# Routing a token layer's experts block by block beside the output projection: router logits taken from the first sublayer's sum

## The chip, the core and the metric

The kernel runs on one core of a Trainium2 chip. The metric is the device time of one execution in microseconds (us). The core has TensorE (PE in the profile; its weight loads are PEld), VectorE (DVE), ScalarE (ACT), GpSimd (POOL) and SyncE (SP), which here only issues transfers. SP and ACT each have a queue of transfers of their own, POOL has one for gathers and scatters.

## The reference, cut to what matters

One layer works on 640 tokens of 1024 numbers: 128 context tokens (modulation vector `c_ctx`) and 512 latent tokens (vector `c`). Sublayer 1 mixes tokens, and sublayer 2 is a mixture of 32 experts of which each token uses two:

```python
sh1, sc1, gt1, sh2, sc2, gt2 = _adaln(c, w_ada[l], b_ada[l])
h = _modulate(xs, g_pre1[l], sh1, sc1)
out, _, _ = _token_mix(h, *mix_w, tabs, cache_ckv[:, l], cache_krope[:, l])
xs = xs + gt1 * _rmsnorm(out, g_post1[l])
h = _modulate(xs, g_pre2[l], sh2, sc2)          # _rmsnorm(x, g) * (1.0 + scale) + shift
xs = xs + gt2 * _rmsnorm(_hier_moe(h, *moe_w), g_post2[l])
...
g_top, g_idx = lax.top_k(g_prob, 1)             # the best of 4 groups
e_top, e_idx = lax.top_k(jax.nn.softmax(e_sel, axis=-1), TOP_K)   # the best 2 of its 8 experts
```

`g_prob` and `e_sel` come from `h @ w_rg + b_rg` and `h @ w_re + b_re`, 4 and 32 columns.

## The kernel before, in words

All arithmetic on TensorE is in 32-bit floats, for which each matmul of the source is two instructions in the profile. The program is one function, `hybrid_layer`, with a block of code for each engine; the engines meet at semaphores. TensorE's work is a list of named groups (`pe_groups`): each takes one of four places of two PSUM banks in turn (n % 4), waits with `begin` until the place's earlier user has been read, and reports with `done`. `landed(eng, name)` waits for a group's end, `free` and `emptied` say and wait that it was read.

The stages: projections, convolution (on DVE) and latent attention up to some 318 us; then, by the list `POST`, the output projection of the five token blocks of 128 (`P0` to `P4`, L1449, 16 matmuls of 512 columns each) with what follows it; then the router's choice; then the experts.

After `P{b}` ACT squares it (L840), DVE scales and adds it to the token rows `x` (L1066, L1068: now x holds the first sublayer's sum), ACT squares that (L849), DVE multiplies by the norm and by `a2`, the scale of sublayer 2 (L1074), and POOL adds the shift `b2` (L568), for the last block DVE (L1079). The result h2 goes to DRAM (L463, L822), from where experts gather it. TensorE transposes it (`ht{b}`, L1270), multiplies by the router's weights (`rt{b}`, L1461) and transposes the logits back (`rl{b}`). These follow the projections by one to three blocks; the last of them come after `P4`. `a2` and `b2` are read from DRAM by SP (L457, L458) once the last attention group `O3` has landed.

When all logits are there DVE picks experts for all five blocks at once in some 45 small steps, each behind a drain (L1104 to L1126), TensorE counts each token's place within its expert (`pos`, L1472), DVE turns the places into one-hot tables (L1145), TensorE makes from them the lists of token numbers (`table0`, L1483), DVE writes them as integers (L1164 to L1169), and POOL gathers the rows of the first pairs of experts (L571). `table1` lists the tokens beyond 64 of an expert.

Experts go in 16 pairs, 64 tokens each: gathered rows are transposed, gate and up matmuls (L1502), silu on ACT, product on DVE, transposes, down matmuls (L1515), copy (L1212), scatter (L576). An expert with more than 64 tokens has extra rounds. A pair's weights (6.3 MB in three pieces) go into one of three slots. SP issues the load of pair p only when pair p - 3 has been used (`w_used`, L1549). Pairs 0 and 1 (without its down piece) are loaded before the projection's end, pair 2 is issued when `P4` has landed, pair 1's down piece when the last h2 is made.

## Time and profile before

| | |
|---|---|
| three runs | 736.33, 736.13, 735.31 us (median 736.13) |
| the profiled execution | 733.19 us, span 731.4 us |
| mean granted TensorE clock | 0.94 |
| PE busy | 592.8 us (81% of the span) |
| DVE, ACT, POOL busy | 267.3, 147.1, 93.8 us |
| chain that ended last | PE 59%, DMA 21%, DVE 7%, issue 5%, ACT 3% |
| moved by DMA | 169.15 MB, mean 231 GB/s |

The span is from the first to the last instruction of the profiled execution. A start time in a row counts from the span's start. A busy share is an average over stages with different limits; what ended the idle time of an engine stands in brackets behind a row of the timeline.

### The profile page before, as it was taken

The numbers are of one execution on the slowest core, as the hardware profiler recorded it, in microseconds if no ns is written. First come the engines' busy times: TensorE is split into PE (matmuls) and PEld (weight loads), VectorE is DVE, ScalarE is ACT, GpSimd is POOL, SyncE is SP. The second block draws the span as 40 slices with busy tenths as digits, with TensorE's granted clock in tenths as the row PEclk, the third lists the DMA queues.
The fourth block names the chain that finished last, engine by engine and source line by source line (L and its number), as shares of the span: only waits on it lengthen the run. The fifth ranks groups of instructions, "written<-read, shape, count | busy, mean of one in ns | idle before, by whom it ended". The sixth has DMA issues, their size and how long they took to land.

```text
span 731.4 us, 8068 instructions
## 1 busy us (share of the span) xinstructions
PE 592.8 (81%) x3086; PEld 304.1 (42%) x3087; DVE 267.3 (37%) x451; ACT 147.1 (20%) x296; POOL 93.8 (13%) x102
## 2 busy tenths in 40 slices
PE   0889899999999999989999267878988777878700
PEld 0656566555555455544455223334333332322200
DVE  2316899998540244402333531101101000100137
ACT  3220000012315444402223102100110000100042
POOL 5000001500000000001110044011111111110015
PEclk9999999999999999999999769989999998999955
DMA  9999935000008510054005720799999999999273
GB/s 334 345 362 369 365 120 198 13 0 1 0 1 353 218 70 1 1 191 181 30 29 228 289 69 30 278 413 405 423 425 424 423 426 427 425 426 407 99 307 144
DMA packets 48548, 169.15 MB, mean 231 GB/s; under 512 B 5642, under 2 KB 14187, under 8 KB 36218
## 3 DMA queue, kind: packets, MB, share of 16 engines
q1 hardware_dynamic: 41216, 156.11, 53.7%
q0 software_dynamic: 6016, 10.96, 4.2%
q10 hardware_dynamic: 1274, 1.52, 0.6%
q8 instruction: 26, 0.43, 0.2%
q14 instruction: 16, 0.13, 0.1%
HBM read 161.48 MB, written 14.44 MB: 241 GB/s over the span
## 4 chain that ended last, share of the span: by engine, by line
PE 59%; DMA 21%; DVE 7%; issue 5%; ACT 3%; PEldq 1%; PEld 1%; DVEq 1%; SPq 1%; ACTq 1%; POOLq 0%
DMA arena<-in_w_up 14%; PE ps L1265 13%; PE ps L1449 9%; PE ps L1502 9%; PE ps L1424 5%; PE ps L1270 4%; PE ps L1515 4%; PE ps L1266 4%; DMA arena<-in_w_ada 3%; PE ps L1433 3%; PE ps L1283 2%; DVE arena L1249 2%; PE ps L1349 2%; DMA x<-in_x_sample 2%; PE ps L1403 1%
## 5 line engine op out<-in xcount | busy, mean ns | idle before, releaser
L1502 PE MATMUL ps<-arena 128*64 128x512 f32 x544 | 129.3, 628 | 22.5 <-DMA arena<-in_w_up 18.0
L1265 PE MATMUL ps<-arena 128*128 128x512 f32 x256 | 131.4, 595 | 1.2 <-issue 1.2
L984 DVE SCALAR_TENSOR_TENSOR arena<-arena 128x655 f32<-128x655 f32 x116 | 95.0, 897 | 0.4 <-issue 0.2
L1502 PEld LDWEIGHTS ps<-arena 128*64 128x64 f32 x544 | 45.5, 145 | 105.1 <-issue 97.2
L1270 PE MATMUL ps<-cst,arena 128*128 128x128 f32 (+2 forms) x349 | 54.7, 300 | 33.0 <-DVE arena L923 17.5
L1515 PE MATMUL ps<-arena 128*64 128x512 f32 x272 | 64.1, 614 | 16.4 <-ACT arena L862 15.8
L1266 PEld LDWEIGHTS ps<-arena 128*128 128x128 f32 x256 | 48.6, 190 | 61.2 <-issue 61.2
L1449 PE MATMUL ps<-arena 128*128 128x512 f32 x160 | 69.2, 593 | 0.9 <-ACT arena L814 0.9
L1270 PEld LDWEIGHTS ps<-cst,arena 128*128 128x128 f32 (+2 forms) x349 | 45.1, 179 | 51.3 <-issue 41.1
L1207 DVE TENSOR_TENSOR arena<-arena,ps 128x256 f32<-128x256 f32 x16 | 6.7, 422 | 132.0 <-ACT arena L867 119.1
L1212 DVE COPY arena<-ps 128x1024 f32<-128x1024 f32 x16 | 19.6, 1225 | 92.6 <-PE ps L1515 92.6
L1266 PE MATMUL ps<-arena 128*128 128x128 f32 (+1 forms) x256 | 50.9, 280 | 0.0
L1449 PEld LDWEIGHTS ps<-arena 128*128 128x128 f32 x160 | 30.2, 190 | 37.9 <-issue 37.9
L867 ACT ACTIVATE arena<-ps 128x256 f32<-128x256 f32 x16 | 6.1, 384 | 191.7 <-PE ps L1502 191.7
L1265 PEld LDWEIGHTS ps<-arena 128*128 128x128 f32 x256 | 39.4, 192 | 2.5 <-issue 2.1
L576 POOL DMA_INDIRECT y_d<-arena,ids x16 | 16.0, 1000 | 187.2 <-DVE arena L1212 186.9
L1424 PE MATMUL ps<-arena 128*128 128x128 f32 (+1 forms) x144 | 39.3, 417 | 0.7 <-ACTq L787 0.7
L568 POOL TENSOR_TENSOR arena<-arena 128x1024 f32<-128x1024 f32 x4 | 9.4, 2342 | 236.4 <-DVE arena L1074 236.4
L1515 PEld LDWEIGHTS ps<-arena 128*64 128x64 f32 x272 | 18.6, 140 | 50.3 <-issue 36.7
L1043 DVE TENSOR_REDUCE amax<-ps 128x1 f32<-128x640 f32 (+1 forms) x20 | 14.3, 717 | 53.9 <-PE ps L1424 53.9
L1424 PEld LDWEIGHTS ps<-arena 128*128 128x128 f32 x144 | 22.5, 191 | 16.8 <-issue 15.3
L862 ACT ACTIVATE arena<-ps 128x1024 f32<-128x1024 f32 (+1 forms) x34 | 22.3, 701 | 33.4 <-PE ps L1270 33.4
(239 smaller groups left out, 523.7 us busy)
## 6 DMA issues: line engine op xcount, KB each, us to landing
arena<-in_w_gate SPq DMA_DIRECT2D x16, 2048.0 KB, 19.8
arena<-in_w_up SPq DMA_DIRECT2D x16, 2048.0 KB, 26.0
arena<-in_w_down SPq DMA_DIRECT2D x16, 2048.0 KB, 30.7
arena<-in_w_ada SPq DMA_DIRECT2D x12, 2048.0 KB, 14.1
arena<-y_d SPq DMA_DIRECT2D x10, 512.0 KB, 7.0
arena<-in_w_in SPq DMA_DIRECT2D x8, 512.0 KB, 13.0
arena<-in_w_out SPq DMA_DIRECT2D x1, 4096.0 KB, 12.9
arena<-ada_d SPq DMA_DIRECT2D x8, 512.0 KB, 10.5
```

The costliest lines, as they stand in the source:

```text
L576: gp.indirect_dma_start(y_d, bass.IndirectOffsetOnAxis(places, 0), src, None, bounds_check=2 * T - 1, oob_is_err=False).then_inc(inc, 16)
L862: return act.activation(dst.rearrange("p k t -> p (k t)"), bank.rearrange("p a b -> p (a b)")[:, 0:count], ACT.Copy)
L984: ins = dve.scalar_tensor_tensor(dst, src, w, dst, ALU.mult, ALU.add)
L1212: dve.tensor_copy(ys[:, s, :], ps[:, 2 + 2 * s:4 + 2 * s, :].rearrange("p a b -> p (a b)")).then_inc(e_ys, 1)
L1265: mm(pp(name)[:, 0:TS], lhs(k), rhs_s(k), start=k == 0, stop=k == steps - 1)
L1266: last = mm(pp(name)[:, 512:512 + width], lhs(k), rhs_p(k), start=k == 0, stop=k == steps - 1)
L1270: return nc.tensor.transpose(out, in_, ident[0:n, 0:n])
L1424: last = mm(g[:, lo:hi], a[:, h, cols], keys, start=m == 0, stop=m == 1)
L1433: mm(g[:, 0:TS], vv[:, 1 + t, n * DV:(n + 1) * DV], pT[:, t, :], start=t == 0, stop=t == 4)
L1449: last = mm(pp(name)[:, half * 512:(half + 1) * 512], mixT[:, k, b * P:(b + 1) * P], wo[:, k, half * 512:(half + 1) * 512], start=k == CM, ...
L1502: last = mm(ps[a:a + ROWS, s, :], src[:, k, a:a + ROWS], slots[w][:, j, 0:2, k * FE:(k + 1) * FE], start=k == 0, stop=k == KD - 1)
L1515: last = mm(ps[a:a + ROWS, 2 + 2 * s + half, :], src[:, k, a:a + ROWS], slots[w][:, j, 2, k * D + half * 512:k * D + (half + 1) * 512], st ...
```

## The change

It computes the router's logits from x, the sum of the first sublayer, instead of from h2. Since h2 = x * r * a2 + b2, with r the row's norm factor, the logits are r * (x @ (a2 * w)) + (b2 @ w + bias). POOL multiplies the router's weights by a2 beforehand, once per modulation vector (`wr0` for block 0, `wr` for the others); TensorE turns a2 and b2 into columns (group `turn34`, after `q1`), multiplies b2 by the weights (`rb`), and spreads the result over 128 partitions (`small`, ahead of `P0`), from where DVE copies it (`biasrow`). So that rows match, the router's weights are read as (k p) instead of (p k).

`P0` to `P4` alternate between places 0 and 1, `ht` keeps place 3, and place 2 holds logits, places, counts and tables. Transposes of x, logits, the choice of experts, the places and the tables now go one block at a time, put between the matmuls of the next projection; the last projection is done column half by column half. The token numbers are built in PSUM with 4096 as a start value, so that DVE's conversion is two operations. ACT makes the numbers. POOL adds b2 for all five blocks; ACT issues the last store. Pair 1's and pair 2's down pieces are loaded after the second gather has landed; the gather of pair 3 is issued in pair 0 instead of pair 1. The wait for `cnt_ready` moves from ahead of pair 0 to behind its down matmuls.

The diff, cut to its core:

```diff
-POST = ["P0", "P1", "P2", "ht0", "P3", "rt0", "ht1", "P4", "rl0", "rt1", "ht2", "ht3", "rl1", "rt2", "rl2", "rt3",
-        "rl3", "ht4", "rt4", "rl4"]
-
-BETWEEN = (("rl0", "rt1", "ht2"), ("ht3", "rl1", "rt2", "rl2", "rt3", "rl3"))
+POST = ["small", "P0", "P1", "ht0", "P2", "ht1", "P3", "ht2", "P4", "ht3", "ht4"]
+HOME = {"small": 2, **{f"P{b}": b % 2 for b in range(NT)}, **{f"ht{b}": 3 for b in range(NT)}}
...
-            load_pair(2, 2)
-            sp.wait_ge(h2_last, 1)
+            load_pair(2, 2, pieces=range(2))
+            sp.wait_ge(h2_ready, NT)
+            sp.wait_ge(xg_in[1], 16)
             load_pair(1, 1, pieces=range(2, 3))
-
+            load_pair(2, 2, pieces=range(2, 3))
...
+            emptied(gp, "rb")
+            gp.wait_ge(proj_dve, 1)
+            gp.tensor_tensor(wr0, wr[:], a2T[:, :, 0:1].broadcast_to([P, KD, G + E]), ALU.mult)
+            gp.tensor_tensor(wr[:], wr[:], a2T[:, :, 1:2].broadcast_to([P, KD, G + E]), ALU.mult)
+            for v in range(2):
+                last = gp.tensor_scalar(diag[:, v, :], ident[0:G + E, 0:G + E], lgb[:, v:v + 1], None, ALU.mult)
+            last.then_inc(wr2_ready, 1)
...
-                if 0 < pair < PAIRS - 2:
+                if pair == 0:
+                    gp.wait_ge(e_tr, 2)
+                    gather(xg[:, 1, :], idg[:, 0, 3:4], xg_in[1])
...
-            act.dma_start(x_rg, i["w_rg"][0].rearrange("(p k) e -> p k e", k=KD)).then_inc(wr_in, 16)
-            act.dma_start(x_re, i["w_re"][0].rearrange("(p k) e -> p k e", k=KD)).then_inc(wr_in, 16)
+            act.dma_start(x_rg, i["w_rg"][0].rearrange("(k p) e -> p k e", p=P)).then_inc(wr_in, 16)
+            act.dma_start(x_re, i["w_re"][0].rearrange("(k p) e -> p k e", p=P)).then_inc(wr_in, 16)
...
+            dve.wait_ge(bias_in, 1)
+            dve.tensor_copy(biasrow, bias_ps).then_inc(bias_ready, 1)
...
+                if n == 1:
+                    begin(pe, "turn34")
+                    pe.wait_ge(rows_ready, 5)
+                    for a in range(4):
+                        last = turn(pp("turn34")[:, a * P:(a + 1) * P], rows[:, 6 + a, :])
+                    done(last, "turn34")
...
+            pe.wait_ge(wr_ready, 1)
+            begin(pe, "rb")
+            for k in range(KD):
+                last = mm(pp("rb")[0:G + E, 0:2], wr[:, k, :], b2T[:, k, :], start=k == 0, stop=k == KD - 1)
+            done(last, "rb")
```

The new code of DVE between the projections (`step` is a drain; the last block, done in halves, is left out):

```python
            def route(b):
                v = min(b, 1)
                Lg, Le = L[:, 0:G], L[:, G:]
                best0, best1, best2 = (m[:, b:b + 1] for m in (m0, m1, m2))
                dve.wait_ge(lg_done, b + 1)
                step(dve.scalar_tensor_tensor(L, lg_ps[:, b, :], stat[:, 7, b:b + 1], biasrow[:, v, :], ALU.mult, ALU.add))
                first_best(pen, Lg, hitg, best0, rankg, 1e30)
                step(dve.scalar_tensor_tensor(em.rearrange("p (g e) -> p g e", g=G), pen.unsqueeze(2).broadcast_to([P, G, EG]), -1e30,
                                              Le.rearrange("p (g e) -> p g e", g=G), ALU.add, ALU.add))
                first_best(oh[:, 0, b, :], em, hit, best1, ranke)
                step(dve.scalar_tensor_tensor(em, oh[:, 0, b, :], -2e30, em, ALU.mult, ALU.add))
                first_best(oh[:, 1, b, :], em, hit, best2, ranke)
                dve.tensor_scalar(rt_e[:, b, 0:G], Lg, best0, None, ALU.subtract).then_inc(mask_ready, 1)
                dve.tensor_tensor(rt_e[:, b, G:], best2, best1, ALU.subtract)
            def find(b):
                dve.wait_ge(pos_done, b + 1)
                for c in range(2):
                    dve.scalar_tensor_tensor(junk[:, c, :], pos_ps[:, b, :], 1.0, oh[:, c, b, :], ALU.mult, ALU.mult, accum_out=at[:, c, b:b + 1])
                dve.drain()
                for c in range(2):
                    last = dve.tensor_scalar(place1[:, c, b, :], iota, at[:, c, b:b + 1], None, ALU.is_equal)
                last.then_inc(place_ready, 1)
            for b in range(NT - 1):
                v = min(b, 1)
                name = f"P{b}"
                dve.wait_ge(pss, b + 1)
                dve.tensor_tensor(po[:], pp(name), gg1[:, v, :], ALU.mult)
                dve.wait_ge(psd, b + 1)
                step(dve.reciprocal(stat[:, 5, b:b + 1], stat[:, 5, b:b + 1]))
                free(dve.scalar_tensor_tensor(x[:, b, :], po[:], stat[:, 5, b:b + 1], x[:, b, :], ALU.mult, ALU.add), name)
                dve.drain().then_inc(x1_ready, 1)
                if b:
                    find(b - 1)
                dve.wait_ge(xsd, b + 1)
                step(dve.reciprocal(stat[:, 7, b:b + 1], stat[:, 7, b:b + 1]))
                if b >= 2:
                    dve.wait_ge(h2_st[b % 2], 16 * (b // 2))
                dve.scalar_tensor_tensor(h2[:, b % 2, :], x[:, b, :], stat[:, 7, b:b + 1], a2[:, v, :], ALU.mult, ALU.mult).then_inc(h2m_ready, 1)
                if b == NT - 2:
                    dve.wait_ge(pss, NT)
                    dve.tensor_tensor(po[:, 0:512], pp(f"P{b + 1}")[:, 0:512], gg1[:, 1, 0:512], ALU.mult)
                    dve.tensor_scalar(stat[:, 1, b + 1:b + 2], stat[:, 0, b + 1:b + 2], 1.0 / D, EPS, ALU.mult, ALU.add).then_inc(rest_ready, 1)
                route(b)
            find(NT - 2)
...
```

The new code of TensorE (turn_rows is 8 transposes of x, logits 8 matmuls of 36 columns, places 2(b+1) and table 8 small ones in bf16; each waits for what its name needs, table(n, b) for number_ready):

```python
            begin(pe, "small")
            pe.wait_ge(wr2_ready, 1)
            for v in range(2):
                last = mm(bias_ps[:, v, :], ones[0:G + E, :], diag[:, v, :], start=True, stop=True)
            last.then_inc(bias_in, 1)
            pe.wait_ge(wo_in, 16)
            pe.wait_ge(bias_ready, 1)
...
            for b in range(NT):
                name = f"P{b}"
                begin(pe, name)
                if b == 0:
                    for h in range(H):
                        emptied(pe, f"O{h}")
                tiles = (*range(CM, KD), *range(CM))
                if b < NT - 1:
                    steps = [(k, half) for k in tiles for half in range(2)]
                else:
                    steps = [(k, half) for half in range(2) for k in tiles]
                for n, (k, half) in enumerate(steps):
                    if b == 0 and k == 0:
                        pe.wait_ge(mixc_ready, CM)
                    if b >= 2 and n == 2:
                        pe.wait_ge(place_ready, b - 1)
                        table(0, b - 2)
                    if b and n == 6:
                        turn_rows(b - 1)
                    if b and n == 9:
                        logits(b - 1)
                    if b and n == 15:
                        places(b - 1)
                    last = mm(pp(name)[:, half * 512:(half + 1) * 512], mixT[:, k, b * P:(b + 1) * P],
                              wo[:, k, half * 512:(half + 1) * 512], start=k == CM, stop=k == CM - 1)
                    if b == NT - 1 and n == 7:
                        last.then_inc(p_half, 1)
                done(last, name)
            turn_rows(NT - 1)
            pe.wait_ge(place_ready, NT - 1)
            table(0, NT - 2)
            logits(NT - 1)
            places(NT - 1)
            pe.wait_ge(place_ready, NT)
            table(0, NT - 1)
            for a in range(NT):
                for c in range(2):
                    last = mm(cnt_ps, onesb[:], oh[:, c, a, :], start=a == c == 0, stop=a == NT - 1 and c == 1)
            last.then_inc(cnt_done, 1)
            pe.wait_ge(place_ready, NT + 1)
            for b in range(NT):
                table(1, b)
```

How TensorE's order changes at the start of the projection. Before, from the last matmul of `O3` (L1434) on into `P0`, `P1` and `P2` (L1449):

```order
L1434 MATMUL ps<-arena 128x128
L1449 MATMUL ps<-arena 128x512 [waits drained1,drained2,drained0,wr_ready,wo_in]
L1449 MATMUL ps<-arena 128x512 x7
L1449 MATMUL ps<-arena 128x512 [waits mixc_ready]
L1449 MATMUL ps<-arena 128x512 x7
```

The same place in the change (L1505 is the end of `O3`, L1583 is `P0`):

```order
L1505 MATMUL ps<-arena 128x128
L1510 MATMUL ps<-cst,ones 128x36 [waits wr2_ready,drained2]
L1510 MATMUL ps<-cst,ones 128x36
L1583 MATMUL ps<-arena 128x512 [waits drained3,drained0,drained2,bias_ready,wo_in]
L1583 MATMUL ps<-arena 128x512 x7
L1583 MATMUL ps<-arena 128x512 [waits mixc_ready] x2
```

And DVE's side of it in the change, between the last attention step (L1110) and the first block's scaling (L1163):

```order
L1110 TENSOR_SCALAR arena<-arena,asum 128x128
L1116 COPY cst<-ps 128x72 [waits b2_in,bias_in,a2_in,gg1_in]
L1163 TENSOR_TENSOR arena<-ps,arena 128x1024 [waits pss]
L1165 RECIPROCAL stat<-stat 128x1 [waits psd]
L1166 SCALAR_TENSOR_TENSOR x<-arena,stat,x 128x1024
```

`P0` now waits for `bias_ready`, which that copy gives, and the copy waits for the loads of a2 and b2.

TensorE in the change from the end of `P1` (L1583) to the logits of block 1; before, sixteen rows of L1449 stood here with nothing between them:

```order
L1543 MATMUL ps<-arena,trib 128x32 [waits mask_ready]
L1543 MATMUL ps<-arena,trib 128x32
L1583 MATMUL ps<-arena 128x512
L1583 MATMUL ps<-arena 128x512 [waits drained0]
L1583 MATMUL ps<-arena 128x512
L1552 MATMUL ps<-padb,onesb 64x16 [waits number_ready,place_ready]
L1555 MATMUL ps<-number,place 64x16 x4
L1552 MATMUL ps<-padb,onesb 64x16
L1555 MATMUL ps<-number,place 64x16 x4
L1583 MATMUL ps<-arena 128x512 x4
L1329 MATMUL ps<-cst,x 128x128 [waits x1_ready,drained3]
```

And DVE in the change after `P1` has landed, up to where it gives `place_ready` for block 0 (second instruction of L1156):

```order
L1163 TENSOR_TENSOR arena<-ps,arena 128x1024 [waits pss]
L1165 RECIPROCAL stat<-stat 128x1 [waits psd]
L1166 SCALAR_TENSOR_TENSOR x<-arena,stat,x 128x1024
L1153 SCALAR_TENSOR_TENSOR arena<-ps,arena 128x32 [waits pos_done]
L1153 SCALAR_TENSOR_TENSOR arena<-ps,arena 128x32
L1156 TENSOR_SCALAR place<-cst,arena 128x64 x2
```

The table of block b - 2 stands behind two matmuls of `P{b}`, and on DVE the place of that block stands behind the scaling of `P{b-1}`.

## Rows read from the trace of the kernel before

**Rows 1.** The page: PE's busy tenths in 40 slices of the span.
```profile
PE   0889899999999999989999267878988777878700
```
**Rows 2.** Timeline of PE at the projections: start, length, engine, line, count, [idle before].
```profile
319.13 31.14 PE L1449 MATMUL ps<-arena 128*128 128x512 f32 x72 [0.95 <-ACT arena L814]
...
375.11 1.94 PE L1461 MATMUL ps<-arena,wr 128*36 128x128 f32 x16
376.98 1.16 PE L1270 MATMUL ps<-cst,arena 128*128 128x128 f32 x8
377.98 13.90 PE L1449 MATMUL ps<-arena 128*128 128x512 f32 x32
```
**Rows 3.** Timeline of SP at attention's end; then L458's issues, us to landing.
```profile
318.21 0.32 SPq L457 DMA_DIRECT2D arena<-ada_d  x1
...
319.52 0.43 SPq L458 DMA_DIRECT2D arena<-ada_d  x1
...
DMA to landing us min/median/max: 5.1/6.2/7.3
```
**Rows 4.** Timeline of DVE and POOL after P3's end at 375.11.
```profile
376.36 0.15 DVE L1062 TENSOR_SCALAR stat<-stat 128x1 f32<-128x1 f32 x1 [8.19 <-ACT arena L840]
...
377.02 1.28 DVE L1066 SCALAR_TENSOR_TENSOR arena<-ps,stat,arena 128x1024 f32<-128x1024 f32 x1
...
382.87 2.35 POOL L568 TENSOR_TENSOR arena<-arena 128x1024 f32<-128x1024 f32 x1 [12.27 <-DVE arena L1074]
```
**Rows 5.** Timeline from the choice of experts to the first expert matmuls.
```profile
407.78 0.17 DVE L1104 TENSOR_REDUCE arena<-cst 128x5 f32<-128x20 f32 x1 [7.00 <-ACT cst L831]
408.03 0.18 DVE L1105 TENSOR_TENSOR arena<-cst,arena 128x20 f32<-128x20 f32 x1
...
418.91 0.72 PE L1483 MATMUL ps<-number,place 128*64 128x32 bf16 x20 [3.12 <-DVE place L1145]
...
421.44 0.18 DVE L1169 TENSOR_TENSOR idg<-arena 128x16 int32<-128x16 f32 x1
...
422.49 1.10 POOL L571 DMA_INDIRECT arena<-h_d,idg  x1 [37.28 <-DVE idg L1169]
...
423.33 0.17 DVE L1181 TENSOR_REDUCE arena<-arena 1x16 f32<-1x32 f32 x1
...
425.98 0.17 DVE L1164 COPY arena<-ps 128x32 f32<-128x32 f32 x1
...
427.00 1.94 PE L1270 MATMUL ps<-cst,arena 128*128 128x128 f32 x8 [2.71 <-DMA arena<-h_d,idg]
...
430.14 9.35 PE L1502 MATMUL ps<-arena 128*64 128x512 f32 x32 [1.20 <-ACT arena L862]
```
**Rows 6.** The page's DMA issues of h2 (count, KB, us to landing), and ACT's queue (packets, MB, share).
```profile
h_d<-arena SPq DMA_DIRECT2D x4, 512.0 KB, 2.6
...
h_d<-arena ACTq DMA_DIRECT2D x1, 512.0 KB, 8.4
...
q10 hardware_dynamic: 1274, 1.52, 0.6%
```
**Rows 7.** Stretches: length, busy PE, PEld, DVE, ACT, POOL, clock, DMA share, GB/s.
```profile
25.00:30.00 5.00, 3.55 (x108) 3.00 (x99) 1.32 (x4) 0.59 (x2) 0.00 (x0) 1.00 0.78 255
...
525.00:550.00 25.00, 22.28 (x108) 8.52 (x106) 2.84 (x4) 3.36 (x6) 3.23 (x4) 1.00 1.01 424
```
**Rows 8.** Timeline of SP and PE among the experts: pair 3's load, and a late gather.
```profile
461.67 0.39 SPq L429 DMA_DIRECT2D arena<-in_w_gate  x1
...
485.62 2.22 PE L1270 MATMUL ps<-cst,arena 128*128 128x128 f32 x10 [3.31 <-DMA arena<-h_d,idg]
```
**Rows 9.** Timeline of PE: gate and up matmuls of a pair after stops of three lengths.
```profile
580.05 7.34 PE L1502 MATMUL ps<-arena 128*64 128x512 f32 x32 [2.90 <-DMA arena<-in_w_up]
...
613.30 9.94 PE L1502 MATMUL ps<-arena 128*64 128x512 f32 x32 [3.44 <-DMA arena<-in_w_up]
...
646.46 8.72 PE L1502 MATMUL ps<-arena 128*64 128x512 f32 x32 [3.29 <-DMA arena<-in_w_up]
```

More of the change, by code:

```diff
@@ L503, in _ @@
             gp.memset(ids[:], PAD)
+            gp.memset(padb[:], float(PAD // P))
             gp.memset(rows, 0.0)
@@ new lines, in _ @@
+            find(NT - 2)
+            b = NT - 1
+            name = f"P{b}"
+            dve.wait_ge(pss, NT + 1)
+            dve.tensor_tensor(po[:, 512:], pp(name)[:, 512:], gg1[:, 1, 512:], ALU.mult)
+            dve.wait_ge(psd, NT)
+            step(dve.reciprocal(stat[:, 5, b:b + 1], stat[:, 5, b:b + 1]))
+            for half in range(2):
+                part_ = slice(512 * half, 512 * (half + 1))
+                ins = dve.scalar_tensor_tensor(x[:, b, part_], po[:, part_], stat[:, 5, b:b + 1], x[:, b, part_], ALU.mult, ALU.add)
+                if half:
+                    free(ins, name)
+                    dve.drain().then_inc(x1_ready, 1)
+                else:
+                    ins.then_inc(x1_ready, 1)
@@ L1184, in _ @@
             step(dve.tensor_scalar(extra[:, 0:PAIRS], extra[:, 0:PAIRS], ROWS.bit_length() - 1, None, ALU.arith_shift_right))
-            runs = [rt[0:1, 8, 2 * n * PAIRS:2 * (n + 1) * PAIRS] for n in range(2)]
-            dve.memset(rt[0:1, 8, 0:4 * PAIRS], 0.0)
-            step(None)
+            for run in runs:
+                last = dve.memset(run, 0.0)
+            step(last)
             step(dve.tensor_copy(runs[0][:, PAIRS:], extra[:, 0:PAIRS]))
@@ new lines, in logits, with places @@
+            def logits(b):
+                if b == NT - 1:
+                    pe.wait_ge(xT_half, 1)
+                else:
+                    emptied(pe, f"ht{b}")
+                for k in range(KD):
+                    if b == NT - 1 and k == KD // 2:
+                        emptied(pe, f"ht{b}")
+                    last = mm(lg_ps[:, b, :], x1T[:, k, :], (wr if b else wr0)[:, k, :], start=k == 0, stop=k == KD - 1)
+                last.then_inc(lg_done, 1)
+            def places(b):
+                pe.wait_ge(mask_ready, b + 1)
+                steps = [(trib if a == b else onesb, c, a) for a in range(b + 1) for c in range(2)]
+                for n, (w, c, a) in enumerate(steps):
+                    last = mm(pos_ps[:, b, :], w[:], oh[:, c, a, :], start=n == 0, stop=n == len(steps) - 1)
+                last.then_inc(pos_done, 1)
@@ new lines, in table @@
+            def table(n, b):
+                pe.wait_ge(number_ready, b + 1)
+                for j in range(2):
+                    at_rows = slice(j * ROWS, (j + 1) * ROWS)
+                    if b == 0:
+                        mm(tables[n][at_rows], onesb[:, 0:ROWS], padb[:], start=True, stop=False)
+                    for c in range(2):
+                        for kind in range(2):
+                            last = mm(tables[n][at_rows], place1[:, c, b, :], number[:, c, b, kind, j::2],
+                                      start=False, stop=c == kind == 1 and b == NT - 1)
+                if b == NT - 1:
+                    last.then_inc(tab_done, 1)
@@ L1488, in _ @@
+            for b in range(NT):
+                table(1, b)
             for s in range(4):
-                n = sum(1 for name in order if place[name][0] == s)
+                n = homes.count(s) - (s == HOME["small"])
                 pe.wait_ge(drained[s], n)
```

397 lines of the change are left out of this document (186 added, 211 removed).

## The prediction

> **What bounds the kernel now.** I read the page first, then the chain of waits, then the timeline of each engine from the end of attention to the first expert, and last the expert stage by stretches. The page's PE row shows TensorE full from the fifth slice to the twentieth and at the ninth tenth again in slices 16 to 21, with one hole, the slice with a 2 [rows 1]. That hole is the router's choice. In it the chain leaves TensorE and runs over DVE, TensorE, DVE, POOL's gather and back. Ahead of it TensorE streams the five output projections almost without a stop: 0.4325 us for each of 160 instructions (31.14 / 72), 13.84 us a block [rows 2]. So whatever is put between them on TensorE is paid in full.
>
> Behind the hole the experts' weights decide. SP issues pair 3's load at 461.67, when pair 0 is used up [rows 8], and from about there DMA is full at 424 GB/s [rows 7]. Thirteen pairs of 6.3 MB have to pass after that moment, so the end of the kernel moves with the start of pair 0, one to one. That start is 430.14 now, 38.3 us after `P4`'s end at 391.88 [rows 2, 5]. All I have to find is when pair 0 starts.
>
> **The change, part by part.** *Ahead of the projections.* `turn34` adds four transposes, at 1.16 / 8 = 0.145 us each 0.6 us [rows 2]. `rb` adds 16 instructions with 2 moving columns. The nearest row takes 1.94 / 16 = 0.12 us with 128 columns; I take half of it, 0.9 us, with nothing and 1.9 as bounds. Both stand in the full stretch [rows 1]: **+1.5**. The copies on ACT and the three small POOL jobs (two products of 288 columns, the diagonals) run under attention, where POOL stands idle; without that cover they would cost about 2 us.
>
> The router's weights now arrive in runs of 16 and 128 bytes, 2048 of them for 256 before. ACT's queue had 1274 packets in 0.6% of 16 engines' span, 55 ns each, so 1792 more cost at most 6 us of DMA [rows 6]. DMA has room just after, a share of 0.78 from 25 to 30 us [rows 7]. I take 0 and keep +4 for the range. The Trainium skill (DMA: Bandwidth & Descriptors, section Why small descriptors are slow) speaks against such runs; by it this load alone would be slower, which no row here shows.
>
> *The wait ahead of P0.* `P0` starts at 319.13 now, once ACT has read `O3` [rows 2]. In the change TensorE first waits for `bias_ready`, DVE's copy, and that copy stands behind DVE's waits for a2 and b2. SP issues these loads at 318.21 to 319.52 and can't sooner, since it waits for `O3` as well; the last of b2 lands up to 7.3 us after issue, at 326.8 [rows 3]. Before, nobody needed them until the first block was squared 14 us later. With 0.3 us for the copy `P0` starts 8.0 us late: **+8.0**. With the shortest landing, 5.1, it would be 5.8. Queued behind this wait is all of TensorE's projection, and all engines wait for that.
>
> TensorE then comes out of 9 us without work. The first expert matmuls, which start after such a hole, took 9.35 us [rows 5], against 7.34 after a short stop [rows 9]. **+2.0** (1.4 to 2.6, rows 9's other two).
>
> *Work put into the projections.* Before, 72.75 us from `P0`'s start to `P4`'s end less 5 x 13.84 leave 3.55 for transposes and logits [rows 2]. Now four blocks have 1.16 for transposes and 1.94 for logits (16 instructions as before, with 128 weight columns and 36 moving instead of the reverse; between 1.0 and 2.2 by the transposes' row), 12.4 us. 20 small matmuls for places and 26 for tables at 0.72 / 20 = 0.036 us [rows 5] add 1.7. Net **+10.5** (7 to 12).
>
> *The wait for a place in the table.* `table(0, b-2)` stands behind the second matmul of `P{b}`, 4 x 0.4325 = 1.73 us after `P{b-1}` has ended. It waits for `place_ready` of block b - 2, which DVE gives only behind the scaling of block b - 1. By rows 4 DVE starts 1.25 us after a projection ends; a product of 1.28, reciprocal and drain 0.25, a second product of 1.28, a drain of 0.15, and four small operations of the place, 0.7, give 4.9 [rows 4]. TensorE stands for 3.15 us in each of `P2`, `P3` and `P4`: **+9.5** (8.4 to 10.5). After it nothing else is late: transposes, ACT's copy, logits and choice each are ready 1 us or more ahead of their turn.
>
> Does a stop of 3.15 us cost the clock? In rows 9 a stop of 2.90 us is followed by 7.34 us, one of 3.29 by 8.72, one of 3.44 by 9.94. Mine lies between the first two, nearer to the one that loses 1.4. I take 0.7 each: **+2.1**, with 0 and 3 x 2.6 = 7.8 as bounds. The Trainium skill (TensorE: Matmul & The Clock Gate, Part 1: The HAM clock gate) says that an idle TensorE falls to half its clock, and that the moment at which it changes varies from run to run. By that each stop could lose 2.6 and the sum below would be 5.7 higher.
>
> *The tail.* With T the end of `P4`: half a row squared, 0.75; scaled and added, 2.35 and 3.0 for the two halves (each 0.65, half of 1.28); squares' sum 4.0; ACT's root behind its two copies 4.65; h2 without shift 6.25 [rows 4]. The choice is 15 drained steps of 0.25 us [rows 5], to 10.3. Places 0.5, DVE's table 0.7, eight matmuls and latency 0.5, the integers 0.45: 12.45, and POOL issues the gather 0.85 later as from 421.62 to 422.49 [rows 5], at 13.3. The store of h2 has to be there too: POOL's add takes 2.35 [rows 4], so it is issued at 9.1 and lands 2.6 to 8.4 later [rows 6]. Pair 2's first 4.2 MB, issued at T, take 10 us at 424 GB/s, so I expect it at 13.3 as well. The gather lands at 17.8 (422.49 to 427.00). TensorE is not ready then: `table1` now stands ahead of the transposes, behind DVE's counting (2.65 us from 423.33 to 425.98, plus 0.45 for a copy and a memset), two big comparisons 1.15, and 42 small matmuls 1.5 [rows 5], to 18.5. Add 3.14 (427.00 to 430.14) and pair 0 starts at T + 21.7, not T + 38.3: **-16.6** (-19 to -13).
>
> *Among the experts.* The moved gather of pair 3 removes a stop of 3.3 us at 485.62 [rows 8]. DMA was full through it, so the loads gain nothing: 0. The down pieces moved behind the second gather (4.2 MB, 10 us) are done 20 us before pair 0 is used up: 0. If they were late, pair 1 would wait.
>
> **The sum.** 1.5 + 8.0 + 2.0 + 10.5 + 9.5 + 2.1 - 16.6 = +17.0 us. The profiled execution had 733.19, so 750.2; the median of the runs shown is 2.94 above it, so I forecast **753.1 us**, own range 747 to 759.
>
> **The rivals.** A: each stop of `P2` to `P4` falls fully to the half clock. For it: rows 9. Against it: my stop is the shortest but one. +22.7, 758.8 us.
>
> B: the expert stage is bound by TensorE early on, not by DMA, and the earlier gather gives back 3.3 us and about 2.5 of slow clock behind it. Against: the DMA share of 1.01. +11.2, 747.3 us.
>
> C, the other side: neither wait shows. `P0` isn't held because b2 is there before `O3` has been read, and the place of a block is ready within 1.73 us of the next landing. Then only work and tail count: 1.5 + 10.5 - 16.6 = -4.6, 731.5 us. For it: the shorter tail is real. Against: SP's issue and DVE's order, both fixed in the program. It decides where `bias_ready` comes before 319.4 and `place_ready` before T' + 1.7.
>
> D: the small runs of the router's weights delay the first chunks: +4 more, 757 us.
>
> **How the numbers follow.** Forecast 0.56, A 0.15, B 0.12, C 0.06, D 0.06, others 0.05. The range 742 to 764 leaves out C and the far ends. About 0.2% (1.5 us) is what a measurement tells from no change. Faster 0.07 (C and a little), same 0.02, slower 0.91.
>
> **What would show it.** In the changed profile `P0` (L1583) starts near 328.6 with an idle of some 9 us ended by DVE's copy L1116; three stops of about 3 us ahead of L1552 or L1555, ended by DVE L1156; `P4` ends near 425.5; the gather (L611) is issued 13 us later; pair 0 starts 22 us after `P4`'s end, and from it on the stage takes as long as before. I am wrong if `P0` starts before 322, if those stops are under 1 us, or if the span from pair 0's start to the end changes by over 3 us.

## The result, and the profile after

The changed kernel takes 756.71 us (median of 4 runs, 755.28 to 760.35), the kernel before 735.72 beside it: ratio 1.030, interval 1.027 to 1.032. The forecast was 753.1 with a range of 742 to 764. The profiled execution took 757.97 with a span of 756.2, so 24.8 more than the profiled one of before, where the sum had +17.0. Between the medians the change costs 21.0: the profiled execution of before lay 2.5 under the median of its four, the profiled one of the change 1.3 above. The table below splits up the 24.8 of the two profiles.

First the page. The columns are 40 slices of the span, as in [rows 1]: busy tenths of PE, then the granted clock in tenths.

```profile
PE   0889899999999999859888848888987787787700
...
PEclk9999999999999999979989957999998999898955
```

The hole of [rows 1], the 2 and the 6, has become one slice with a 4, the 24th. It is shorter, as meant. In its place the stretch ahead of it, from the 18th slice on, has a 5 and eights where nines stood. These are the new waits. The timeline of PE names them (start, length, engine, line, operation, count, idle before it and what ended that):

```profile
322.13 0.63 PE L1510 MATMUL ps<-cst,ones 36*128 36x36 f32 x4 [0.85 <-ACT arena L862]
330.43 21.46 PE L1583 MATMUL ps<-arena 128*128 128x512 f32 x44 [7.67 <-issue]
...
368.12 0.20 PE L1552 MATMUL ps<-padb,onesb 128*64 128x16 bf16 x1 [3.13 <-DVE place L1156]
...
368.43 5.40 PE L1583 MATMUL ps<-arena 128*128 128x512 f32 x8
...
390.45 0.40 PE L1555 MATMUL ps<-number,place 128*64 128x16 bf16 x8 [3.48 <-DVE place L1156]
390.78 6.57 PE L1583 MATMUL ps<-arena 128*128 128x512 f32 x8
...
413.68 0.39 PE L1555 MATMUL ps<-number,place 128*64 128x16 bf16 x8 [3.12 <-DVE place L1156]
414.00 5.21 PE L1583 MATMUL ps<-arena 128*128 128x512 f32 x8
...
429.64 1.10 PE L1583 MATMUL ps<-arena 128*128 128x512 f32 x2
433.24 1.51 PE L1329 MATMUL ps<-cst,x 128*128 128x128 f32 x8 [2.50 <-DVE x L1191]
...
435.01 3.63 PE L1535 MATMUL ps<-wr,arena 128*128 128x36 f32 x16
443.58 0.40 PE L1543 MATMUL ps<-arena,onesb 128*128 128x32 bf16 x8 [4.94 <-DVE arena L1146]
...
452.37 1.94 PE L1329 MATMUL ps<-cst,arena 128*128 128x128 f32 x8 [1.05 <-DMA arena<-h_d,idg]
455.51 5.39 PE L1617 MATMUL ps<-arena 128*64 128x512 f32 x12 [1.20 <-ACT arena L918]
```

`P0` (L1583) starts 7.67 us after the bias matmuls. "Issue" stands there because DVE's copy is so short. DVE's own timeline has it, behind a wait for the load of a2 and b2:

```profile
330.10 0.23 DVE L1116 COPY cst<-ps 128x72 f32<-128x72 f32 x1 [16.44 <-DMA arena<-ada_d]
```

Then come three stops of 3.1 to 3.5 us ahead of the tables, and behind each, eight instructions of projection in 5.2 to 6.6 us instead of 8 x 0.4325 = 3.5 [rows 2]. The stretches (columns as in [rows 7]) tell why they are slow:

```profile
331.00:335.00 4.00, 4.00 (x6) 1.52 (x5) 0.00 (x0) 0.00 (x0) 0.00 (x0) 0.50 1.01 426
...
368.00:374.00 6.00, 5.88 (x22) 2.79 (x23) 1.51 (x3) 0.64 (x3) 2.34 (x1) 0.72 0.08 33
390.00:397.00 7.00, 6.54 (x16) 2.97 (x17) 1.85 (x4) 0.98 (x3) 2.34 (x1) 0.53 0.19 74
413.00:420.00 7.00, 6.32 (x25) 3.48 (x26) 2.00 (x8) 1.20 (x3) 2.34 (x1) 0.76 0.14 57
434.00:452.00 18.00, 7.23 (x98) 6.41 (x97) 11.55 (x69) 3.81 (x9) 4.63 (x3) 0.50 0.70 264
```

The third number from the end is the granted clock: 1.00 is 2.4 GHz and 0.50 is 1.2 GHz; a value between them is the mean of a stretch that holds both. It is 0.53 to 0.76 behind the three stops, and 0.50 in the tail from 434 us on. What holds the place back is DVE's order around the first stop, as the prediction had it: block 1's product and scaling stand ahead of the place of block 0, whose last comparison (L1156) releases TensorE.

```profile
364.46 1.23 DVE L1163 TENSOR_TENSOR arena<-ps,arena 128x1024 f32<-128x1024 f32 x1 [2.81 <-ACT arena L874]
...
365.83 1.28 DVE L1166 SCALAR_TENSOR_TENSOR x<-arena,stat,x 128x1024 f32<-128x1024 f32 x1
...
367.65 0.42 DVE L1156 TENSOR_SCALAR place<-cst,arena 128x64 bf16<-128x64 f32 x2
```

Against [rows 5], pair 0 now starts 24.8 us after `P4`'s end at 430.74, not 38.3. It starts at 455.51 instead of 430.14, and from there to the end of the span it is 300.7 us against 301.3. SP issues pair 3's load 31.8 us after pair 0's start, 31.5 before [rows 5, 8].

The 24.8 us by the prediction's terms, each from these rows or from an experiment below:

| term | forecast | measured |
|---|---|---|
| ahead of attention's end | +1.5 | +3.1 (321.31 against 318.21), mostly scatter |
| wait ahead of P0 | +8.0 | +8.2 (9.12 from SP's issue of a2 to P0, against 0.92) |
| clock behind it | +2.0 | +2.3 |
| work among the projections | +10.5 | +9.0 |
| three stops | +9.5 | +9.7 |
| clock behind them | +2.1 | +6.1 |
| tail | -16.6 | -13.5 |
| experts | 0 | -0.6 |

They add to 24.3; 0.5 lies in the gaps between the groups.

### The profile page after: what moved, and what is told of

It reads as the page before. It is cut to its first block and busy times, and to the rows that moved or that the text cites. A ratio compares the mean times of both kernels' runs of the same rounds, so it can differ in the third digit from the quotient of the medians.

```text
span 756.2 us, 8386 instructions
## 1 busy us (share of the span) xinstructions
PE 609.3 (81%) x3169; PEld 309.4 (41%) x3170; DVE 277.0 (37%) x538; ACT 151.0 (20%) x311; POOL 97.8 (13%) x108
## 3 DMA queue, kind: packets, MB, share of 16 engines
q10 hardware_dynamic: 3066, 1.52, 0.7%
## 5 line engine op out<-in xcount | busy, mean ns | idle before, releaser
L1617 PE MATMUL ps<-arena 128*64 128x512 f32 x544 | 133.6, 648 | 24.4 <-DMA arena<-in_w_up 19.5
L1324 PE MATMUL ps<-arena 128*128 128x512 f32 x256 | 132.1, 598 | 1.1 <-issue 1.1
L1617 PEld LDWEIGHTS ps<-arena 128*64 128x64 f32 x544 | 43.0, 148 | 113.8 <-issue 110.6
L1583 PE MATMUL ps<-arena 128*128 128x512 f32 x160 | 80.6, 656 | 7.7 <-issue 7.7
L1630 PE MATMUL ps<-arena 128*64 128x512 f32 x272 | 62.1, 598 | 16.9 <-ACT arena L918 15.9
L1325 PEld LDWEIGHTS ps<-arena 128*128 128x128 f32 x256 | 48.8, 191 | 61.5 <-issue 61.5
L1329 PE MATMUL ps<-cst,arena 128*128 128x128 f32 (+1 forms) x313 | 48.5, 297 | 26.7 <-DVE arena L981 17.5
L1329 PEld LDWEIGHTS ps<-cst,arena 128*128 128x128 f32 (+1 forms) x313 | 40.0, 176 | 43.7 <-issue 39.4
L1583 PEld LDWEIGHTS ps<-arena 128*128 128x128 f32 x160 | 32.4, 211 | 43.5 <-issue 43.4
L616 POOL DMA_INDIRECT y_d<-arena,ids x16 | 15.8, 989 | 195.1 <-DVE arena L1271 185.7
L1324 PEld LDWEIGHTS ps<-arena 128*128 128x128 f32 x256 | 39.6, 193 | 2.7 <-issue 2.3
L1630 PEld LDWEIGHTS ps<-arena 128*64 128x64 f32 x272 | 18.1, 136 | 49.2 <-issue 35.6
L607 POOL TENSOR_TENSOR arena<-arena 128x1024 f32<-128x1024 f32 x5 | 11.7, 2342 | 198.1 <-DVE arena L1174 179.1
L1495 PEld LDWEIGHTS ps<-arena 128*128 128x128 f32 x144 | 22.5, 191 | 16.8 <-issue 15.3
## 6 DMA issues: line engine op xcount, KB each, us to landing
arena<-in_w_in SPq DMA_DIRECT2D x8, 512.0 KB, 12.8
arena<-in_w_out SPq DMA_DIRECT2D x1, 4096.0 KB, 12.6
arena<-ada_d SPq DMA_DIRECT2D x8, 512.0 KB, 10.3
```

Of the source, the lines that this page charges most:

```text
L616: gp.indirect_dma_start(y_d, bass.IndirectOffsetOnAxis(places, 0), src, None, bounds_check=2 * T - 1, oob_is_err=False).then_inc(inc, 16)
L1324: mm(pp(name)[:, 0:TS], lhs(k), rhs_s(k), start=k == 0, stop=k == steps - 1)
L1325: last = mm(pp(name)[:, 512:512 + width], lhs(k), rhs_p(k), start=k == 0, stop=k == steps - 1)
L1329: return nc.tensor.transpose(out, in_, ident[0:n, 0:n])
L1495: last = mm(g[:, lo:hi], a[:, h, cols], keys, start=m == 0, stop=m == 1)
L1583: last = mm(pp(name)[:, half * 512:(half + 1) * 512], mixT[:, k, b * P:(b + 1) * P], wo[:, k, half * 512:(half + 1) * 512], start=k == CM, ...
```

## The experiments

**One wait alone.** DVE copies the bias row first.

```diff
-            dve.wait_ge(gg1_in, 32)
-            dve.wait_ge(a2_in, 32)
-            dve.wait_ge(b2_in, 32)
             dve.wait_ge(bias_in, 1)
             dve.tensor_copy(biasrow, bias_ps).then_inc(bias_ready, 1)
+            dve.wait_ge(gg1_in, 32)
+            dve.wait_ge(a2_in, 32)
+            dve.wait_ge(b2_in, 32)
```

> The changed kernel with one edit: DVE copies the bias row ahead of its waits for gg1, a2 and b2, so TensorE's bias_ready no longer hangs on those loads. Theory (the wait ahead of P0 and the slow clock behind it are both its doing): P0's first matmul starts near 322.5 instead of 330.43 and P0 takes 13.9 us instead of 16.3, so the time falls by 8 + 2.5 = 10.5 us, to about 746 us. Rival (P0 is slow because of the two small matmuls and the single-precision work before it, not the idle): P0 still takes 16 us, the time falls by 8 us only, to about 749. Second rival (the b2 load is waited for elsewhere, by DVE's scaling of block 0): under 4 us fall. The three stops for place_ready stay at 3.1 to 3.5 us in all of these.

743.36 us, ratio 1.0116 (1.0088 to 1.0144): 13.4 us below the changed kernel. PE's timeline:

```profile
322.72 0.63 PE L1510 MATMUL ps<-cst,ones 36*128 36x36 f32 x4 [0.85 <-ACT arena L862]
323.72 19.12 PE L1583 MATMUL ps<-arena 128*128 128x512 f32 x44 [0.37 <-issue]
...
359.07 0.20 PE L1552 MATMUL ps<-padb,onesb 128*64 128x16 bf16 x1 [3.13 <-DVE place L1156]
```

The wait is gone and the 44 instructions take 19.12 instead of 21.46, so the slow clock was the wait's doing: 2.3 us. `P0` starts 1.8 us after SP's issue of a2, 0.9 more than before the change: that much of the 8.2 are the two bias matmuls. The stops stand as they were, at 3.13, 3.48 and 3.12 us, and the groups behind them take 5.40, 6.25 and 5.05 us. The wait and its clock explain 9.6 us. The two profiled executions are 12.7 apart, and 3.0 of that lie behind pair 0's start (297.7 us to the end), in a stage that this edit does not touch and that varies by as much from run to run (below).

**The stops alone.** DVE makes the place ahead of the square's wait.

```diff
                 name = f"P{b}"
+                if b:
+                    find(b - 1)
                 dve.wait_ge(pss, b + 1)
...
                 dve.drain().then_inc(x1_ready, 1)
-                if b:
-                    find(b - 1)
```

> The changed kernel with one edit: in the block loop DVE makes the place of block b-1 before it waits for the square of projection b, not after block b is scaled. Theory (stops and the slow clock behind them belong together, rival A of the prediction): the three stops of 3.13, 3.48 and 3.12 us go, and the eight instructions behind them take 3.5 us instead of 5.4, 6.6 and 5.2, together 9.7 + 6.8 = 16.5 us less, about 740 us. Rival (the slow clock comes from the many small matmuls of tables and places between the projections): 9.7 us less, about 747. Second rival (the place is then late for another reason, since places(b-1) ends only 0.4 us before the projection): DVE's scaling starts later, under 8 us less.

738.95 us, ratio 1.0065 (1.0042 to 1.0089): 17.8 below the changed kernel. All three stops are gone, and behind each table there is now

```profile
361.86 3.70 PE L1583 MATMUL ps<-arena 128*128 128x512 f32 x8
...
378.87 3.70 PE L1583 MATMUL ps<-arena 128*128 128x512 f32 x8
```

at a granted clock of 1.00. Against 3.70, the groups of the changed kernel lost 1.7, 2.9 and 1.5 us. The small matmuls of places and tables are still there, so they don't lower the clock; the stops do. Rival A's mechanism was right, and most of its size: 6.1 of the 7.8 us that it took for three stops.

**Both edits together**, measured twice.

> Both edits together. Theory (the two waits and their clock are the whole loss): 10.5 + 16.5 = 27 us less than the changed kernel, about 730 us, so 6 us (0.8%) faster than the kernel before. Rival (with the waits gone another wait takes their place, DVE or ACT as the bound of the block loop): over 734. From pair 0's start to the end 300 to 302 us either way.

730.22 us, ratio 0.9939 (0.9919 to 0.9960). The second time:

> e3_both_early once more, in more rounds, beside the other three: 0.994 of the kernel before. If it is within 0.2% of it, the first result was scatter of the part ahead of the projections, which came out at 318 or at 321 us in kernels whose code is the same up to there.

729.79 us, ratio 0.9927 (0.9898 to 0.9956). So 27 us of loss were two orders of DVE's instructions, and without them the change is 0.6 to 0.7% faster than the kernel before: small, but both intervals end below 1. This kernel also gives the price of the work alone: from `P0`'s start at 319.30 to `P4`'s end at 401.07 it is 81.77 us, against 72.75 [rows 2], so 9.0.

**The wait alone in the kernel before.**

```diff
                             emptied(pe, f"O{h}")
+                        pe.wait_ge(b2_in, 32)
```

> The kernel before with one wait added and nothing else: TensorE waits for the b2 load ahead of P0. Theory: P0 starts 7.5 us late (by the landing at 326.8 instead of 319.13) and runs its first instructions at the lower clock, 2.5 us more: +10, about 746 us. Rival (no clock is lost behind such a hole): +7.5, about 743. Second rival (the expert stage gives it back, since its end is set by the weight loads and not by pair 0's start): under +4.

743.45 us, ratio 1.0106 (1.0071 to 1.0141), 8.9 more than before. Its row:

```profile
328.87 44.09 PE L1450 MATMUL ps<-arena 128*128 128x512 f32 x96 [8.21 <-DMA arena<-ada_d]
```

The idle of 8.21 was 0.95 before [rows 2], and 96 instructions at 0.4325 take 41.5: 7.3 + 2.6 = 9.9, and the interval is 5 to 10 us. Nothing downstream gives the wait back: from pair 0's start to the end it is 301.2 us, 301.3 without the added wait.

**The tail: traffic.** Here and below the edits stand on the kernel with both early edits. Pair 2's loads wait for the last h2 store:

```diff
             landed(sp, f"P{NT - 1}")
+            sp.wait_ge(h2_st[0], 16 * 3)
             load_pair(2, 2, pieces=range(2))
-            sp.wait_ge(h2_ready, NT)
```

> The kernel with both early edits (e3_both_early), and pair 2's gate and up loads issued only when the last h2 store has landed. There the gather was issued at 417.88, 1.3 us after its indices; ready indices alone gave 0.87 in the kernel before. Theory (the store, slowed by these 4.2 MB, ended last): the store lands in about 3 us instead of 6.6, the gather is issued 0.45 us earlier, pair 0 starts 0.45 us earlier, the time falls by 0.5 us, under what can be measured. Rival (the loads come too late for pair 2): pair 2's gate and up waits, over 1 us slower.

734.05 us, ratio 0.9999 (0.9973 to 1.0025): 4 us slower than both edits alone. Neither theory had the reason, which the timelines of SP, POOL and PE show:

```profile
413.34 0.38 SPq L457 DMA_DIRECT2D arena<-in_w_gate  x1
...
417.57 1.14 POOL L611 DMA_INDIRECT arena<-h_d,idg  x1 [7.13 <-DVE idg L1213]
...
426.57 1.94 PE L1329 MATMUL ps<-cst,arena 128*128 128x128 f32 x8 [4.15 <-DMA arena<-h_d,idg]
```

The store landed 2.8 us after its issue at 410.47 and the gather was issued 0.4 us earlier after `P4`'s end, as the theory had it, but now 4.2 MB lay in front of it. From the gather's issue to TensorE's start it took 9.0 us, against 4.5 in [rows 5] and in the kernel with both edits. Pair 0 started 28.5 us after `P4`'s end instead of 24.5. The loads don't hold up the gather when they are issued at `P4`'s end, some 16 us ahead of it: with both edits alone the last of them lands at 415.88, and the gather is issued at 417.88.

With the loads behind both gathers instead, and pair 1's down pieces first:

```diff
             landed(sp, f"P{NT - 1}")
-            load_pair(2, 2, pieces=range(2))
             sp.wait_ge(h2_ready, NT)
             sp.wait_ge(xg_in[1], 16)
             load_pair(1, 1, pieces=range(2, 3))
-            load_pair(2, 2, pieces=range(2, 3))
+            load_pair(2, 2)
```

> The kernel with both early edits (e3_both_early), and pair 2's gate and up loads issued behind both first gathers, after pair 1's down pieces, so that neither the last h2 store nor the gather has other traffic beside it. 8.4 MB at 424 GB/s need 20 us, to 445, and pair 2 reads them at 456, so they should not be missed. Theory (in e6_store_first the loads collided with the gather, which landed 4.2 us later): the gather lands as in e3_both_early or 0.5 us earlier, the time is within 1 us of it, about 730. Rival (e6_store_first was slow because pair 2's loads came late): again 4 us slower.

729.28 us, ratio 0.9926 (0.9901 to 0.9950), as both edits alone. The gather was issued 16.4 us after `P4`'s end instead of 16.8 and was no longer waited for, since `table1`, which stands ahead of the transposes, ended as late. So the store that lands last in the tail costs under half a microsecond.

**The tail: clock.** Extra matmuls into a free bank fill TensorE's waits.

```diff
+            def keep_busy(count):
+                for _ in range(count):
+                    mm(ps[:, 2, :], ident, x[:, 0, 0:512], start=True, stop=True)
+            emptied(pe, f"P{NT - 2}")
+            keep_busy(5)
             turn_rows(NT - 1)
...
             logits(NT - 1)
+            keep_busy(9)
             places(NT - 1)
...
             last.then_inc(cnt_done, 1)
+            keep_busy(7)
             pe.wait_ge(place_ready, NT + 1)
```

> The kernel with both early edits, and 21 extra matmuls of 128x512 in a free bank in the tail: 5 ahead of the last block's transposes, 9 behind its logits, 7 behind the counts, each group meant to end before the wait that follows it. Theory (idle stops of 2.5 to 5 us put TensorE at half its clock): logits of block 4 take 1.9 us instead of 3.63, the transposes of pair 0 1.04 instead of 1.94, its gate and up 7.1 instead of 9.48. The gather gains nothing from the logits, since the h2 store ends last: 0.9 + 2.4 = 3.3 us less, about 727. Rival (half clock comes from the kind of work, or the extra matmuls themselves run at half clock and hold up the places): no fall, up to 3 us more. Second rival (the expert stage is bound by the weight loads whose first issue depends on pair 0's end): the whole 3.3 us arrives, for that is what the theory says; if it were bound by loads alone from pair 0 on, 0.

727.94 us, ratio 0.9922 (0.9896 to 0.9947). The experiment was sized badly: each call is two instructions, so the first group ran 4.3 us in a wait of 2.5, and pair 0 started 26.3 us after `P4`'s end, later and not earlier. The time came out as forecast (727), but not by way of the tail. Why it is no longer than with both edits alone stays unexplained: 298.5 us from pair 0 on is among the shorter ones. The same groups with the store first:

> Both of the last two edits. Theory: now the shorter logits count too, since the gather no longer waits for the store: 1.7 + 0.9 + 2.4 + 0.45 = 5.4 us less than e3_both_early, about 725. Rival (store not what holds the gather): as e7_warm.

734.97 us, ratio 1.0012 (0.9989 to 1.0035): the gather collides with pair 2's loads again. With the loads late and groups of 3, 5 and 4:

> As e10_loads_late, with extra matmuls in the tail again, now 3, 5 and 4: in e7_warm each turned out to be two instructions of 0.43 us, so its groups of 5, 9 and 7 ran 1.5 to 3 us over the waits they were to fill. Theory (each idle stop costs clock behind it, and the groups now fit): pair 0 starts 21.5 us after P4's end instead of 24.5 (1.7 from the logits, 0.9 from the transposes, 0.5 from the store), and its gate and up take 7.1 us: 5.5 us less than e3_both_early, about 725. Rival (the extra matmuls still delay what follows): as e7_warm, 728 or more.

727.77 us, ratio 0.991 (0.9889 to 0.9931), the best here, though its interval overlaps that of both edits alone, so a gain of the clock is not shown by the time. The tail's clock, first with both edits alone, where `P4` ended at 401.07:

```profile
404.00:414.00 10.00, 5.40 (x32) 4.90 (x30) 5.63 (x21) 1.56 (x5) 2.34 (x1) 0.50 1.00 413
414.00:424.00 10.00, 4.21 (x78) 3.83 (x78) 7.06 (x56) 2.46 (x6) 2.16 (x2) 0.50 0.34 100
```

then here, where it ended at 403.53, and two rows of PE:

```profile
404.00:414.00 10.00, 9.82 (x47) 5.23 (x45) 7.95 (x18) 2.65 (x8) 2.34 (x1) 1.00 0.11 46
414.00:424.00 10.00, 5.83 (x81) 3.38 (x82) 7.15 (x50) 2.46 (x6) 2.16 (x2) 1.00 0.27 83
```

```profile
407.47 1.97 PE L1534 MATMUL ps<-wr,arena 128*128 128x36 f32 x16
...
426.00 8.72 PE L1624 MATMUL ps<-arena 128*64 128x512 f32 x32 [1.21 <-ACT arena L917]
```

The clock is whole from `P4`'s end to 424 us, the logits take 1.97 instead of 3.63, and pair 0 starts 22.5 us after `P4`'s end. The theory's 21.5 was too good, and gate and up took 8.72 instead of 9.5, not 7.1: they start behind pair 0's transposes and a wait of 1.21 us that no group fills, and there the granted clock is 0.50 again (426 to 428 us).

**The last block's halves.** The last projection writes both halves in turn again, its first product stands behind block 3's place, and the numbers of block 3 ahead of the first square.

```diff
-                if b < NT - 1:
-                    steps = [(k, half) for k in tiles for half in range(2)]
-                else:
-                    steps = [(k, half) for half in range(2) for k in tiles]
+                steps = [(k, half) for k in tiles for half in range(2)]
...
-                    if b == NT - 1 and n == 7:
+                    if b == NT - 1 and n == 14:
```

> The kernel with both early edits, without one part of the change: the last projection again writes both halves in turn, so ACT squares and DVE scales its first half after P4's end and not beside it. Theory: one half square (0.75 us) and one half product (0.65 us) come back on the path in part, pair 0 starts 25.2 to 26 us after P4's end instead of 24.5, about +1 us. Rival (the halves are hidden by the wait for the h2 store): 0.

729.07 us, ratio 0.9913 (0.9883 to 0.9944). Pair 0 starts 24.65 us after `P4`'s end; in the two profiles of both edits it was 24.46 and 24.73. Computing the last projection half by half gives nothing that shows. The halves behind it, of x and its transposes, are still there in this run and were not tried.

**Pair 3's gather** back behind pair 0's scatter:

```diff
-                if pair == 0:
-                    gp.wait_ge(e_tr, 2)
-                    gather(xg[:, 1, :], idg[:, 0, 3:4], xg_in[1])
-                elif 1 < pair < PAIRS - 2:
+                if 0 < pair < PAIRS - 2:
```

> The kernel with both early edits, pair 3's gather back behind pair 0's scatter as in the kernel before. Theory (the stage is bound by its weight loads, so the moved gather gives nothing): the stop of 3.3 us in front of pair 3's transposes comes back, the time stays within 1 us. Rival B of the prediction (bound by TensorE there): 3 to 6 us slower.

733.31 us, ratio 0.9981 (0.9958 to 1.0005): 3 us slower than both edits alone, with intervals that barely touch. The theory, which allowed 1 us, missed. PE and SP:

```profile
483.93 2.20 PE L1326 MATMUL ps<-cst,arena 128*128 128x128 f32 x10 [4.43 <-DMA arena<-h_d,idg]
487.08 5.63 PE L1627 MATMUL ps<-arena 128*64 128x512 f32 x16 [0.96 <-ACT arena L915]
```

```profile
492.98 0.37 SPq L457 DMA_DIRECT2D arena<-in_w_gate  x1
```

A stop of 4.43 us, then a down that takes 5.63 instead of 3.65, and SP issues pair 5's load 64.8 us after pair 0's start. With both edits alone that issue is at 483.24, 57.7 us after it. Pairs 3 and 4 are 12.6 MB, 29.7 us at 424 GB/s, from the issue of pair 3's load at 458.93 to some 489, so DMA runs short before the next load comes. The stretches show it, here and then with both edits alone, as far from pair 0's start:

```profile
490.19:494.19 4.00, 3.53 (x16) 0.96 (x14) 1.23 (x1) 0.00 (x0) 0.00 (x0) 0.88 0.93 365
494.19:500.19 6.00, 6.00 (x30) 1.84 (x26) 0.00 (x0) 0.00 (x0) 2.02 (x2) 1.00 0.89 303
```

```profile
487.53:491.53 4.00, 4.00 (x24) 1.76 (x19) 0.42 (x1) 0.38 (x1) 0.38 (x1) 1.00 1.00 418
491.53:497.53 6.00, 4.54 (x21) 1.55 (x22) 0.43 (x1) 1.30 (x2) 0.00 (x0) 1.00 1.02 427
```

DMA was full during the stop (a share of 1.01 from 479 to 484 us), and ran below its 424 GB/s from some 6 us behind it. The missing 59 and 121 GB/s over 4 and 6 us are 2.3 us of transfer (an estimate from these rows), and the loads stay late: counted from pair 0's start, the last piece of gate and up weights lands at 251.4 us here, at 249.3 and 249.1 in the kernel before and the one with the added wait, and at 245.8 to 247.9 in the eleven profiles with the early gather. From pair 0's start to the end it is 303.4 us here, 301.3 and 301.2 in the kernel before and the one with the added wait, and 297.7 to 300.7 (mean 299.6) in the eleven.

## Why the prediction was right, and where it was off

*The number.* The median, 756.71, is 3.6 above the forecast and 2.1 below rival A's 758.8. So by time alone A stood nearer, and by mechanism too where the two differ, in the clock behind the stops. The own range, 747 to 759, held it with 2.3 us to spare.

*What bounds.* Right: what `P0` and the projections lost or won came through to the end, up to the 3 us by which the expert stage varies, and with both waits removed the time fell by 27 us.

*The wait ahead of P0, +8.0.* Measured 8.2, of which 0.9 are the two bias matmuls and 7.3 the loads. Its place, its cause (DVE's copy behind the loads) and its clock (2.0 against 2.3) held, shown by taking it away and by putting it into the kernel before.

*The three stops, +9.5.* Measured 9.7, for the reason given.

*Their clock, +2.1.* This is the largest miss: 6.1. The step that failed is "mine lies between the first two, nearer to the one that loses 1.4": it read a rule out of three stops in [rows 9] whose loss happened to rise with their length. Length doesn't order the losses in other traces (last section), and 3.13, 3.48 and 3.12 us lost 1.7, 2.9 and 1.5. Three rows that spread from 0 to 2.6 between 2.90 and 3.44 us gave a mean, 3 x (0 + 1.4 + 2.6) / 3 = 4.0, and no interpolation. The base was off too: 7.34 is not the time at full clock, which is 7.09 (last section), so the three rows lost 0.3, 1.6 and 2.9, together 4.7. The Trainium skill (TensorE: Matmul & The Clock Gate, Part 1: The HAM clock gate) says that TensorE falls to half its clock when idle, at a moment that varies; by it every stop could lose the most that [rows 9] show, 5.7 above my term in all. The trace agrees that each of the three stops costs clock, and lies 4.0 above my term.

*Work, +10.5.* Measured 9.0. The busy times of a group, 1.16 for eight transposes and 1.94 for the logits, contain an end that overlaps the next group. From start to start the trace of both edits has 0.88 and 1.71, some 2 us less over four blocks, which covers the miss of 1.5.

*The tail, -16.6.* Measured -13.5, just inside its bounds of -19 to -13. Two steps failed. The sum let the choice start at 6.55 (10.3 less 3.75), behind h2, with the logits taken as ready. They weren't: at half clock they took 3.63, not 1.94, and the choice began 7.9 us after `P4`'s end. It then took 4.9, not "15 drained steps of 0.25 us", 3.75. So it ended at 12.8 instead of 10.3. And the gather was issued at 17.05 instead of 13.3: its indices were there at 15.1, and the last store, issued at 8.8 and landed 7.3 later, held it for about 1 us. And pair 0's transposes waited 1.05 us for the gather, behind a `table1` that ended at 20.6, where the sum had `table1` last, at 18.5. The sum charged half clock behind the wait ahead of `P0`, but not in the tail, where TensorE has more such waits.

*Experts, 0.* In the profiled pair -0.6, but by the late gather some 2 to 4 us of gain. The step "DMA was full through it, so the loads gain nothing" failed: by the rows of the late gather a stop can cost its price later, when the next load is issued late into a queue that has run dry. Rival B had the sign; its mechanism, TensorE as the bound, was not it.

*Ahead of attention, +1.5, and rival D, +4 more.* SP's issue of a2 stood at 318.21 and 320.69 in the two profiles of the kernel before and of the one with the added wait, and at 317.47 to 322.76, mean 320.2, in twelve whose code up to there is that of the change. So the +3.1 of the one pair is mostly scatter and the mean is +0.8, though from only two profiles on the one side. The times say the same: with both edits everything behind that point adds up to 9.0 of work, 0.9 of bias matmuls, -13.7 of tail and -1.7 of experts, -5.5, and both medians are 4.3 under the kernel before. That leaves about +1, not D's +5.5. The Trainium skill (DMA: Bandwidth & Descriptors, Why small descriptors are slow) has such runs slower per byte; ACT's queue did rise from 0.6% [rows 6] to 0.7% of the engines' time at 3066 packets, but no experiment changes the short runs alone, and whether they cost anything at all stays open.

*Rival C* fell: both waits were there in full. Three errors of the same sign (clock +4.0, tail +3.1, the scatter ahead +1.6), one against them (work -1.5) and some small terms make the profiled execution 7.8 us longer than the sum. Between the medians the sum is short by 4.0. The first and largest of them is rival A's mechanism, and the range held because it took A in.

## What to carry to other kernels

Before work is woven into a full TensorE stream, follow each of its inputs through the in-order queue of the engine that makes it: both waits here were one short DVE instruction standing behind long ones that nobody needed yet, and swapping the order turned +3% into -0.6 to -0.7%. Price a stop of some 3 us inside such a stream at more than its length: here the three cost 15.8 us with their clock, for 9.7 of standing still. And where loads are issued on consumption, judge a stop not by DMA's share during it, but by when the next load is issued and when the queue runs dry.

## What the hardware showed unexpectedly

Stops of the same length cost very different clock. In the changed kernel one of 3.43 us ahead of gate and up lost nothing, and one of 3.39 ahead of the same instructions in the same execution lost 2.7:

```profile
637.27 7.09 PE L1617 MATMUL ps<-arena 128*64 128x512 f32 x32 [3.43 <-DMA arena<-in_w_up]
...
653.88 9.82 PE L1617 MATMUL ps<-arena 128*64 128x512 f32 x32 [3.39 <-DMA arena<-in_w_up]
```

Nor does the same length cost the same in another execution. In the one with the bias row copied first, 3.43 us lost 1.7 and 4.00 lost nothing:

```profile
625.27 8.78 PE L1617 MATMUL ps<-arena 128*64 128x512 f32 x32 [3.43 <-DMA arena<-in_w_up]
...
675.63 7.09 PE L1617 MATMUL ps<-arena 128*64 128x512 f32 x32 [4.00 <-DMA arena<-in_w_up]
```

What decides it was not found. With 12 otherwise useless matmuls (24 instructions) in three groups the clock stayed whole through 20 us in which TensorE still stood three times for 0.9 to 2.3 us.

A small gather behind 4.2 MB of weights landed 8.9 us after its issue, and 4.4 without them; a store of 0.5 MB took 2.8 us alone and 7.3 beside them.

And kernels with the same code up to attention's end reach it anywhere from 317.5 to 322.8 us, so that one pair of profiles can't price a change of one or two microseconds ahead of it.
